# Two joints of a two-block transformer kernel, worked by halves of the tokens

## The chip, the cores and the metric

The kernel runs on one NeuronCore of a Trainium2 chip. The metric is the device time of one execution in microseconds (us); the time shown for a kernel is the median of its runs. The engines are called PE (TensorE), DVE (VectorE), ACT (ScalarE), POOL (GpSimd) and SP (SyncE, which here issues the loads).

## The reference

512 tokens of width 1024 go through two blocks, all in float32. The part that matters here begins inside the first block and ends inside the second:

```python
h2 = _modulate(_rmsnorm(x, norm2_g[l]), mod_l[3], mod_l[4])
x = x + mod_l[5] * _conv_ffn(h2, ...)          # its w_down: 2816 -> 1024
...
return _rmsnorm(x, final_norm_g)               # end of the first block
...
h = rms_norm(x, norm_mix_pre[l])               # second block
proj = h @ w_in[l]                             # begins with q and k, 1024 columns
...
x = x + rms_norm(merged @ w_out[l], norm_mix_post[l])
h = rms_norm(x, norm_ffn_pre[l])
u = causal_dwconv(h @ w_up[l], conv_ffn_w[l])  # 1024 -> 5632
a, g = jnp.split(u, 2, axis=-1)
f = (jax.nn.gelu(g, approximate=True) * a) @ w_down[l]
x = x + rms_norm(f, norm_ffn_post[l])
```

Between `w_down` of the first block and `w_in` of the second stand two norms in a row, and between `w_out` and `w_up` of the second stand two norms with a residual sum between them. At each of these joints every number of the next product depends on all 1024 features of its token.

## The kernel before, in words

Activations lie with the features on the 128 partitions, in KC = 8 chunks of 128, and the T = 512 tokens along the free side. A linear produces one block of 128 output features at a time in one PSUM bank of 512 columns. Each product in float32 precision is made of three matmuls (`product`, lines 551 to 554): both operands are split into a high part (float32r) and a low part (the rest), and high x low, low x high and high x high are added. So a block with 1024 inputs is 24 matmuls of 512 columns, and a block of the down projection with its 22 input chunks is 66.

**Weights.** `load_order` is one list of weight tiles of 128 x 1024 (or 896), in the order of use. SP loads each into one of RAW = 3 raw places (`load`, lines 2336 and before) as soon as the low part three tiles earlier is made (`s_lo`). ACT writes the high part (`prepare`, line 1202) and DVE the low part (`low`, line 1676), each into one of KEPT = 3 places; ACT waits for the tile three before to be used up by PE (`s_used`). The places in each engine's program where `prepare(n)` and `low(n)` stand are written by hand, so they are queued between that engine's other work, in order.

**Order.** Every engine runs one program written out in order (`tensor_program`, `scalar_program`, `vector_program`, `gpsimd_program`, `sync_program`), and they meet only through semaphores. Blocks of output rotate through banks 0 to 5 (`turn`), banks 6 and 7 (`NORM_BANKS`) hold norm sums and spread factors. A bank is taken again when what it held has been read (`freed`).

**A norm.** ACT squares the chunks, DVE adds the squares up (`add`, line 1693). PE sums over the partitions by matmuls against a column of ones (`sum_over_partitions`, line 628), which gives one number per token, the tokens on the partitions. ACT takes the root (`root`, line 1214), DVE the reciprocal (line 1697), and PE spreads the factors over a bank by a product with the identity (`spread`, line 642). DVE then multiplies each chunk (`plain`), ACT makes its high part (line 1217) and DVE its low part; PE starts with chunk k when its low part is there.

**Joint one** (before). After the eight down blocks PE forms the sums of the final norm (`n_final`) and of the squares times the final gain (`n_three`), whole. `n_three`'s factor is derived from both sums by DVE (lines 2098 to 2103), spread first, then `n_final`'s. DVE makes the eight chunks of h (lines 2115 and 2108), the first two of the eight q and k linears run side by side, chunk by chunk (`side_by_side`), and x times the final norm is written after that (line 2123).

**Joint two** (before). While the eight output blocks run, ACT squares each and copies it to `y_buf`, DVE adds. Then the sum and spread of `n_post`, `y_buf` times its factor (line 2209), the sum to x (line 2213, and for chunks 1 and 4 on POOL, line 2302), squares of the new x (ACT, line 1619), their addition in pairs on POOL (line 2306), `n_four`'s sum on PE over the pairs, its root and spread, the eight chunks (lines 2224 and 2218), and the first two of 44 up blocks side by side.

**The first block's own joint**, between its output and its up projection, is already by halves of 256 tokens: `half_steps` makes one half of a block with 24 matmuls of 256 columns, `side_by_side_halves` runs several blocks chunk by chunk on one half and calls sums and spreads of the other half between the chunks, and `piece` gives four half-wide places to the normed chunks. Its steps on DVE are lines 1923, 1989, 2001, 2009 and 2015, on ACT 1436, 1441 and 1446.

Of the kernel before, what the change touches and what calls it, by code (L numbers as in the profile page):

```python
# [13 lines left out]
P = 128  # L14
# [37 lines left out]
    ("conv_mix_w_2", AC * 3), ("conv_ffn_w_2", 2 * FC * 3), ("eps", 1), ("one", 1),  # L52
# [19 lines left out]
KEPT = 3  # L72
STICK = 5
# [190 lines left out]
def two_blocks(nc, io, out):  # L264
    with ExitStack() as whole:
# [19 lines left out]
        small = sb(whole, "small", [P, TT])  # L285
        std = sb(whole, "std", [P, 2 * TT])
# [44 lines left out]
        with ExitStack() as branch:  # L331
# [15 lines left out]
            with ExitStack() as merge:  # L347
                m_hi = sb(merge, "m_hi", [P, KC, T], F32R)
                m_lo = sb(merge, "m_lo", [P, KC, T], F32R)
                y_buf = sb(merge, "y_buf", [P, KC, T])  # L350
                pairs = sb(merge, "square_pairs", [P, 4, T])
# [45 lines left out]
        N_TILES = len(loads.tile_load)  # L397
        row_load = [i for i, entry in enumerate(loads.load) if entry[0] == "row"]
# [47 lines left out]
        n_final = NormSems(1)  # L446
        n_three, n_post, n_four = NormSems(0, factor=0), NormSems(1), NormSems(0)
        s_n3_both = semaphore("n3_both")
# [10 lines left out]
        h_one, h_two, h_three, h_four = (InputSems(*n) for n in ((0, 0, 0), (0, 1, 1), (2, 1, 3), (3, 1, 4)))  # L459
# [16 lines left out]
        s_x1f, s_x1n = semaphore("x1_ffn"), semaphore("x1_normed")  # L476
# [7 lines left out]
        s_y, s_yn, s_x2_v, s_x2_p, s_pair = (semaphore(n) for n in ("y", "y_normed", "x2_v", "x2_p", "pair"))  # L484
# [5 lines left out]
        s_y2, s_yn2, s_x3_v, s_x3_p = Count(s_y, KC), Count(s_yn, KC), Count(s_x2_v, KC - 2), Count(s_x2_p, 2)  # L490

        POOL_CHUNKS = (1, 4)

        def by_engine(k, vector, pool):

            if k in POOL_CHUNKS:
                return pool, POOL_CHUNKS.index(k) + 1
            return vector, k + 1 - sum(c < k for c in POOL_CHUNKS)

        def x2_by(k):  # L500
            return by_engine(k, s_x2_v, s_x2_p)
# [34 lines left out]

        def early_at(i):
# [5 lines left out]
        def tensor_program(e):  # L543
# [12 lines left out]
            def tile_of(t):  # L556
                e.wait_ge(s_lo, t + 1)
                return w_hi[:, t % KEPT, :], w_lo[:, t % KEPT, :]

# [416 lines left out]
            for o in range(KC):  # L976
# [3 lines left out]
            turn = (turn + KC) % 6  # L980
# [7 lines left out]
            freed[n_three.bank] = h_three.plain.at(KC)  # L988
            norm_spread(n_final, TT)
            freed[n_final.bank] = (s_x1n, KC)  # L990
# [3 lines left out]
            side_by_side(W["qk2"], (turn, (turn + 1) % 6), h_hi, h_lo, h_three.lo.sem, h_three.lo.chunk)  # L994
            for o in range(2 * AC):
                b = (turn + o) % 6
                if o >= 2:
                    linear(W["qk2"] + o, 1, b, h_hi, h_lo)
                freed[b] = (s_qk2, o + 1)
            turn = (turn + 2 * AC) % 6  # L1000
# [110 lines left out]
            for o in range(KC):  # L1111
# [3 lines left out]
                freed[b] = (s_y, o + 1)  # L1115
            turn = (turn + KC) % 6
            norm_sum(n_post, exact[:, 0, :], squares[:, 0, :], TT)
            norm_spread(n_post, TT)
            freed[n_post.bank] = (s_yn, KC)
            free(n_four.bank)  # L1120
            for k in range(KC):
                if k >= KC - 2:
                    e.wait_ge(*n_four.square.at(k + 1))
                    done = sum_over_partitions(n_four.bank, pairs[:, k % 4, :], TT, False, k == KC - 1)
                elif k % 2:
                    e.wait_ge(s_pair, k // 2 + 1)
# [1394 lines left out]
```

## Time and profile before

| | |
|---|---|
| median of 3 runs | 1445.42 us (1444.22 to 1450.18) |
| the profiled execution | 1444.88 us |
| its span in the profile | 1443.6 us |
| PE matmuls busy | 1384.5 us, 96% |
| DVE busy | 741.7 us, 51% |
| ACT busy | 598.8 us, 41% |
| POOL busy | 14.3 us, 1% |
| HBM traffic | 103 GB/s over the span |

Times in the rows are microseconds from the span's start, and a matmul's duration includes its way through the array: one starts every 0.23 us though each is shown with 0.39. In the profile's 40 slices of the span PE is at nine tenths or more in all but the first, the last and four others; two of these, the 29th and 30th at seven tenths, are joint two at 1032 to 1081. Joint one is at 665 to 678.

### The profile page before, as it was taken

What the parts mean: (1) busy time and instruction counts of PE and PEld (TensorE: products, weight loads), DVE (VectorE), ACT (ScalarE), POOL (GpSimd) and SP (SyncE); (2) the same over time, 40 slices, a digit from 0 to 9 for tenths busy, and PEclk for the clock granted to TensorE, in tenths of its full rate; (3) what the DMA queues carried; (4) which work ended last, traced back from release to release, by engine and by line L of the source; (5) the groups of instructions that cost most, each with busy time, mean ns of one, the idle gap of its engine ahead of it and who ended that gap; (6) DMA issues with size and microseconds to landing.
All of it is one profiled execution on the core that took longest, in us unless ns stands there. A gap on an engine that the chain in (4) does not pass through costs nothing.

```text
span 1443.6 us, 16617 instructions
## 1 busy us (share of the span) xinstructions
PE 1384.5 (96%) x6734; PEld 1123.9 (78%) x6734; DVE 741.7 (51%) x985; ACT 598.8 (41%) x835; POOL 14.3 (1%) x20
## 2 busy tenths in 40 slices
PE   6999988999999999999999999999779999999997
PEld 3777766888888888887887887888668888888886
DVE  5678855665554443334414444444466566654224
ACT  5646766353333333222344444334343344333221
POOL 0000000000000000000000000000100000000000
PEclk9999999999999999998999999999879999999998
DMA  9644322323432332331322221324103322333331
GB/s 382 260 142 139 108 70 84 106 80 131 140 138 92 98 97 81 99 103 45 106 85 73 74 73 37 95 88 125 65 26 110 99 88 88 102 99 94 94 94 59
DMA packets 43099, 150.41 MB, mean 104 GB/s; under 512 B 4752, under 2 KB 6928, under 8 KB 41872
## 3 DMA queue, kind: packets, MB, share of 16 engines
q1 hardware_dynamic: 42144, 144.76, 30.7%
q0 software_dynamic: 880, 4.59, 1.0%
q8 instruction: 54, 0.88, 0.3%
q14 instruction: 21, 0.17, 0.0%
HBM read 146.45 MB, written 2.10 MB: 103 GB/s over the span
## 4 chain that ended last, share of the span: by engine, by line
PE 90%; DVE 5%; ACT 2%; issue 1%; DMA 1%; POOL 0%; DVEq 0%; SPq 0%; ACTq 0%
PE banks L552 27%; PE banks L554 26%; PE banks L553 26%; PE banks L628 1%; PE banks L693 1%; PE banks L837 1%; PE banks L696 1%; PE banks L704 1%; PE banks L1054 1%; PE banks L1053 1%; PE banks L642 1%; PE banks L820 1%; PE banks L1045 1%; PE banks L1081 1%; PE banks L666 1%
## 5 line engine op out<-in xcount | busy, mean ns | idle before, releaser
L552 PE MATMUL banks<-h_lo,w_hi 128*128 128x512 f32 (+1 forms) x1224 | 480.0, 392 | 9.6 <-DVE h_lo L2015 3.1
L553 PE MATMUL banks<-h_hi,w_lo 128*128 128x512 f32 (+1 forms) x1224 | 475.0, 388 | 0.0
L554 PE MATMUL banks<-h_hi,w_hi 128*128 128x512 f32 (+1 forms) x1224 | 474.9, 388 | 0.0
L1676 DVE TENSOR_TENSOR w_lo<-raw_w,w_hi 128x1024 fp32r<-128x1024 f32 (+2 forms) x229 | 266.2, 1164 | 367.9 <-ACT w_hi L1202 367.4
L1202 ACT ACTIVATE w_hi<-raw_w 128x1024 fp32r<-128x1024 f32 (+2 forms) x229 | 230.1, 1006 | 240.3 <-PE banks L554 214.1
L552 PEld LDWEIGHTS banks<-h_lo,w_hi 128*128 128x128 f32 x1224 | 231.5, 189 | 66.2 <-issue 12.0
L554 PEld LDWEIGHTS banks<-h_hi,w_hi 128*128 128x128 f32 x1224 | 231.5, 189 | 50.5
L553 PEld LDWEIGHTS banks<-h_hi,w_lo 128*128 128x128 f32 x1224 | 231.8, 189 | 48.5
L552 PE MATMUL banks<-a_lo,w_hi 128*128 128x512 f32 (+1 forms) x374 | 142.7, 382 | 0.0
L554 PE MATMUL banks<-a_hi,w_hi 128*128 128x512 f32 (+1 forms) x374 | 142.2, 380 | 0.0
L553 PE MATMUL banks<-a_hi,w_lo 128*128 128x512 f32 (+1 forms) x374 | 141.6, 379 | 0.0
L554 PEld LDWEIGHTS banks<-a_hi,w_hi 128*128 128x128 f32 x374 | 70.2, 188 | 14.8
L553 PEld LDWEIGHTS banks<-a_hi,w_lo 128*128 128x128 f32 x374 | 70.3, 188 | 14.5
L552 PEld LDWEIGHTS banks<-a_lo,w_hi 128*128 128x128 f32 x374 | 70.3, 188 | 13.8
L1745 DVE SCALAR_TENSOR_TENSOR exact<-banks,cols_sb,exact 128x510 f32<-128x510 f32 (+1 forms) x44 | 33.0, 749 | 53.5 <-ACT exact L1635 52.7
L1745 DVE SCALAR_TENSOR_TENSOR normed<-banks,cols_sb,normed 128x510 f32<-128x510 f32 (+1 forms) x66 | 49.2, 746 | 3.2 <-ACT normed L1635 2.4
L1635 ACT ACTIVATE exact<-banks,cols_sb 128x512 f32<-128x512 f32 x22 | 15.2, 689 | 83.1 <-PE banks L554 83.1
L1217 ACT ACTIVATE a_hi<-normed 128x512 fp32r<-128x512 f32 x44 | 27.8, 633 | 47.2 <-DVE normed L2075 30.5
L1739 DVE SCALAR_TENSOR_TENSOR cv_acc<-cv_in,cols_sb,cv_acc 128x512 f32<-128x512 f32 x60 | 45.0, 749 | 1.2
L1923 DVE SCALAR_TENSOR_TENSOR x_res<-banks,mod,x_res 128x512 f32<-128x512 f32 (+1 forms) x23 | 16.1, 702 | 42.0 <-PE banks L554 42.0
L1483 ACT ACTIVATE normed<-normed 128x512 f32<-128x512 f32 x22 | 13.9, 632 | 54.8 <-DVE normed L2071 54.8
L2134 DVE SCALAR_TENSOR_TENSOR sp<-banks,sp 128x1024 f32<-128x1024 f32 (+1 forms) x8 | 11.9, 1492 | 41.9 <-ACT sp L1543 41.9
(284 smaller groups left out, 1411.0 us busy)
## 6 DMA issues: line engine op xcount, KB each, us to landing
raw_w<-in_w_ffn_up SPq DMA_DIRECT2D x44, 512.0 KB, 3.8
raw_w<-in_w_up SPq DMA_DIRECT2D x44, 512.0 KB, 3.8
raw_w<-in_ada_rows SPq DMA_DIRECT2D x24, 512.0 KB, 4.2
early<-in_ada_turned SPq DMA_DIRECT2D x8, 1024.0 KB, 16.3
raw_w<-in_w_gates SPq DMA_DIRECT2D x16, 512.0 KB, 3.6
raw_w<-in_w_ffn_down SPq DMA_DIRECT2D x16, 448.0 KB, 3.3
raw_w<-in_w_down SPq DMA_DIRECT2D x16, 448.0 KB, 3.3
raw_w<-in_w_conv SPq DMA_DIRECT2D x12, 512.0 KB, 3.6
```

The costliest lines, as they stand in the source:

```text
L552: e.matmul(dst, lhs_hi, rhs_lo, start=first, stop=False)
L553: e.matmul(dst, lhs_lo, rhs_hi, start=False, stop=False)
L554: return e.matmul(dst, lhs_hi, rhs_hi, start=False, stop=last)
L628: done = e.matmul(bank[b][:, t:t + 1], part[:, t * P:(t + 1) * P], ones[:, :], start=(first and t == 0), stop=(last and t == nt - 1), skip ...
L642: done = e.matmul(bank[b][:, t * P:(t + 1) * P], f[:, t:t + 1].to_broadcast([P, P]), identity, start=True, stop=True)
L1202: e.activation(w_hi[:, t % KEPT, 0:n], raw[:, i % RAW, 0:n], ACT.Copy).then_inc(s_hi, 1)
L1217: e.activation(dst, src, ACT.Copy).then_inc(done, 1)
L1635: e.activation(dst, bank[b[n]][:, :], ACT.Copy, scale=col("conv_ffn_w_2", w)).then_inc(s_up2_centre.sem, 1)
L1676: e.tensor_tensor(w_lo[:, s, 0:n], raw[:, i % RAW, 0:n], w_hi[:, s, 0:n].bitcast(F32), ALU.subtract).then_inc(s_lo, 1)
L1739: e.scalar_tensor_tensor(out=acc, in0=src, scalar=col("cv_w", i), in1=acc, op0=ALU.mult, op1=ALU.add).then_inc(s_tap_v, 1)
L1745: return e.scalar_tensor_tensor(out=y[:, shift:T], in0=src[:, 0:T - shift], scalar=w, in1=y[:, shift:T], op0=ALU.mult, op1=ALU.add)
L1923: e.scalar_tensor_tensor(out=x[:, o, tok], in0=bank[b][:, 0:tok.stop - tok.start], scalar=mod[:, gate + o:gate + o + 1], in1=x[:, o, tok], ...
```

## The change

At both joints the tokens are worked in two halves, and the sums of both norms of each joint are formed from what is known earlier.

- Joint one: the last down block is made for tokens 0 to 255, then for 256 to 511. The pre-norm's factor is taken from one sum, of squares with the gain sqrt(g^2 + eps), so that the final norm's sum is no longer needed for it. Its sum, root, reciprocal and spread are made per half, the first half's during the second half of the down block. Three linears are made by halves (the first two side by side). The final norm's own sum is moved behind linear three and its spread behind linear four, and x times the final norm after it; low parts of weight tiles stand between its chunks.
- Joint two: the last three output blocks are made first for one half of the tokens, then for the other. The sum of squares of the new x is no longer taken from it: with y the output times its gain and f the post norm's factor, it is the sum of x^2 (from joint one's factors, `x_total`), twice f times the sum of x y, and f^2 times the sum of y^2. So three sums run along with the output blocks: squares of the output, x times y (`cross`, DVE), squares of y. Per half PE sums them over the partitions, and both norms' factors are spread together. Five up blocks run side by side by halves.
- Weights: five more places (`late_hi`, `late_lo`) hold tiles of the output blocks 3 to 7 and of up blocks 3 to 5, in memory that the branches used, so `prepare` and `low` run up to six tiles ahead (`kept_at`).
- POOL no longer takes part in joint two.

The core of the diff (the same pattern for half 1 and plain renumbering of semaphores left out):

```diff
+        def kept_at(t):
+            n, ring = t - W["out2"], KC + 3
+            if n < 3:
+                return (w_hi[:, t % KEPT, :], w_lo[:, t % KEPT, :]), t - KEPT
+            if n < KC or ring <= n < ring + 3:
+                at = n - 3 if n < KC else n - ring
+                return (late_hi[:, at, :], late_lo[:, at, :]), W["out2"] - 1 if n < KC else t - KC
+            at = (W["out2"] + (n - KC if n < ring else n - ring - 3)) % KEPT
+            return (w_hi[:, at, :], w_lo[:, at, :]), t - KC if n < ring else t - 6 if n < ring + 6 else t - KEPT
...
 # PE, joint one
-            norm_sum(n_final, exact[:, 0, :], squares[:, 0, :], TT)
-            norm_sum(n_three, exact[:, 1, :], squares[:, 1, :], TT)
-            e.wait_ge(s_n3_both, 2)
-            spread(n_three.bank, small[:, 0:TT], TT).then_inc(n_three.spread.sem, 1)
-            norm_spread(n_final, TT)
-            side_by_side(W["qk2"], (turn, (turn + 1) % 6), h_hi, h_lo, h_three.lo.sem, h_three.lo.chunk)
+            for k in down_half(0):
+                pass
+            for k in down_half(1):
+                if k == 4:
+                    third_sum(0)
+                elif k == 6:
+                    third_spread(0)
+            tiles, places = [W["qk2"] + n for n in range(3)], [(turn + n) % 6 for n in range(3)]
+            side_by_side_halves(0, tiles[0:2], places, h_three.lo.sem, third_ready, None, {3: third_sum, 6: third_spread})
+            half_linear(tiles[2], places[2], 0, h_hi, h_lo)
+            for t, b in zip(tiles, places):
+                half_linear(t, b, 1, h_hi, h_lo, at=HALF, ready=h_three.lo.sem, need=third_ready, done=s_used)
...
+                if o == 3:
+                    sum_over_partitions(n_final.bank, exact[:, 0, :], TT, True, True).then_inc(n_final.sum.sem, 1)
+                elif o == 4:
+                    norm_spread(n_final, TT)
...
 # PE, joint two
+            for u in range(KC - 3, OUT_UNITS):
+                o, half = (u, 0) if u < KC else (u - 3, 1)
+                for j, _ in enumerate(half_steps(W["out2"] + o, b, half, m_hi, m_lo, done=s_used if half else s_late)):
+                    if (u, j) == (KC, 3):
+                        output_squares(0)
+                    elif (u, j) == (KC, 7):
+                        output_sums(0)
+                    elif (u, j) == (KC + 1, 7):
+                        output_spreads(0)
+            side_by_side_halves(0, tiles, places, h_four.lo.sem, fourth_ready, None, {1: output_squares, 2: output_sums, 6: output_spreads})
+            side_by_side_halves(1, tiles, places, h_four.lo.sem, fourth_ready, s_used, {})
...
 # ACT, per output block or half block
+                e.activation((parts_of if u else totals)[Y_SQUARES][:, tok], src, ACT.Square)
+                e.activation(y_buf[:, o, tok], src, ACT.Copy, scale=col("norm_mix_post_2", o))
+                e.activation((parts_of if u else totals)[SCALED_SQUARES][:, tok], src, ACT.Square, scale=col("norm_mix_post_2", o))
...
 # DVE, joint one
+            add_third(0)
+            add_third_squares(0)
+            third_factor(0)
+            third_plain(0, 0)
+            for k in range(1, KC):
+                third_plain(0, k)
+                third_lo(0, k - 1)
+                if k == 2:
+                    low(W["qk2"] + 1)
+                elif k == 3:
+                    low(W["qk2"] + 2)
+                elif k == 4:
+                    add_third(1)
+                elif k == 5:
+                    add_third_squares(1)
+                    low(W["qk2"] + 3)
...
 # DVE, joint two
+            for o in range(KC - 3):
+                low(W["out2"] + (7, 8, 10, 11, 12)[o])
+                output_unit(o)
+            low(W["up2"] + LATE_KEPT)
+            output_unit(KC - 3)
+            output_unit(KC - 2)
+            cross(KC - 1)
+            post_factor(0)
+            fourth_total(0)
+            fourth_factor(0)
+            output_unit(KC)
+            added_y(0, 0)
+            added_y(0, 1)
+            fourth_plain(0, 0)
+            low(W["up2"] + LATE_KEPT + 1)
+            for k in range(KC - 1):
+                if k + 2 < KC:
+                    added_y(0, k + 2)
+                fourth_plain(0, k + 1)
+                fourth_lo(0, k)
+                if k == 0:
+                    output_unit(KC + 1)
+                elif k == 2:
+                    cross(KC + 2)
+                elif k == 3:
+                    post_factor(1)
+                    fourth_total(1)
+                elif k == 5:
+                    fourth_factor(1)
+            added_y(1, 0)
+            added_y(1, 1)
+            fourth_lo(0, KC - 1)
...
 # POOL
-            add_chunk(1)
-            pair(1)
-            pair(3)
-            add_chunk(4)
-            pair(5)
```

`output_unit(u)` on DVE is one product (`cross`) and three additions into running sums; units 0 to 4 are whole output blocks, 5 to 7 the first halves of the last three and 8 to 10 their second halves. `added_y` multiplies a half chunk of y by the spread factor and then, after that has finished, adds it to x. `fourth_total` is five dependent operations on 128 x 2 elements.

## Rows read from the trace of the kernel before

**Rows 1.** The profile's chain of work that ended last, share of the span by engine.

```profile
PE 90%; DVE 5%; ACT 2%; issue 1%; DMA 1%; POOL 0%; DVEq 0%; SPq 0%; ACTq 0%
```

**Rows 2.** PE's timeline, joint one: start, duration, line, operation [idle before, releaser].

```profile
664.65 0.39 PE L554 MATMUL banks<-a_hi,w_hi 128*128 128x512 f32 x1
...
677.85 0.49 PE L552 MATMUL banks<-h_lo,w_hi 128*128 128x512 f32 x1 [0.68 <-DVE h_lo L2108]
```

**Rows 3.** PE's timeline, joint two.

```profile
1032.25 0.95 PE L628 MATMUL banks<-ones,exact 128*128 128x1 f32 x8
1033.10 1.05 PE L628 MATMUL banks<-ones,squares 128*128 128x1 f32 x8
...
1060.70 0.77 PE L552 MATMUL banks<-h_lo,w_hi 128*128 128x512 f32 x1 [2.32 <-DVE h_lo L2218]
...
1080.55 0.50 PE L552 MATMUL banks<-h_lo,w_hi 128*128 128x512 f32 x1 [1.49 <-DVE w_lo L1676]
```

**Rows 4.** Busy us by stretch: PE, PEld, DVE, ACT, POOL; then PEclk, DMA share, GB/s.

```profile
990.00:1033.00 43.00, 43.00 (x194) 35.40 (x192) 13.20 (x15) 15.64 (x24) 0.00 (x0) 1.00 0.28 94
1033.00:1060.00 27.00, 13.93 (x66) 13.03 (x65) 14.47 (x20) 7.41 (x15) 7.26 (x5) 0.56 0.07 20
1083.00:1200.00 117.00, 117.00 (x505) 94.87 (x504) 69.89 (x84) 46.10 (x61) 0.00 (x0) 1.00 0.32 100
```

**Rows 5.** PE's timeline, the first block's joint, already by halves.

```profile
275.15 0.28 PE L552 MATMUL banks<-h_lo,w_hi 128*128 128x256 f32 x1
...
282.85 0.28 PE L554 MATMUL banks<-h_hi,w_hi 128*128 128x256 f32 x1
284.36 0.58 PE L628 MATMUL banks<-ones,exact 128*128 128x1 f32 x4 [1.22 <-DVE exact L1989]
...
285.94 0.61 PE L642 MATMUL banks<-consts_sb,rstd 128*128 128x128 f32 x4
286.31 0.37 PE L552 MATMUL banks<-h_lo,w_hi 128*128 128x256 f32 x1
...
297.79 0.39 PE L552 MATMUL banks<-h_lo,w_hi 128*128 128x256 f32 x1 [2.11 <-DVE h_lo L2015]
...
300.13 0.41 PE L552 MATMUL banks<-h_lo,w_hi 128*128 128x256 f32 x1
...
302.05 0.41 PE L552 MATMUL banks<-h_lo,w_hi 128*128 128x256 f32 x1
```

**Rows 6.** Timelines of ACT and DVE: steps like the new ones, from four places.

```profile
284.97 0.26 ACT L1441 ACTIVATE std<-banks,cols_sb 128x2 f32<-128x2 f32 x1 [1.22 <-PE banks L628]
285.26 0.17 DVE L2001 RECIPROCAL rstd<-std 128x2 f32<-128x2 f32 x1 [1.05 <-ACT std L1441]
...
302.34 0.48 DVE L2009 SCALAR_TENSOR_TENSOR normed<-x_res,gain,banks 128x256 f32<-128x256 f32 x1
302.73 0.48 DVE L2015 SCALAR_TENSOR_TENSOR h_lo<-normed,mod,h_hi 128x256 fp32r<-128x256 f32 x1
...
650.41 1.28 DVE L1693 TENSOR_TENSOR exact<-exact,squares 128x512 f32<-128x512 f32 x2
...
998.80 0.60 ACT L1209 ACTIVATE exact<-banks 128x512 f32<-128x512 f32 x1 [5.38 <-PE banks L554]
999.30 0.59 ACT L1611 ACTIVATE y_buf<-banks 128x512 f32<-128x512 f32 x1
...
1434.75 0.48 DVE L2274 SCALAR_TENSOR_TENSOR y_buf<-y_buf,cols_sb,banks 128x256 f32<-128x256 f32 x1 [0.81 <-PE banks L642]
1435.26 0.42 DVE L2278 TENSOR_TENSOR x_res<-x_res,y_buf 128x256 f32<-128x256 f32 x1
1435.61 0.86 DVE L2274 SCALAR_TENSOR_TENSOR y_buf<-y_buf,cols_sb,banks 128x256 f32<-128x256 f32 x2
```

**Rows 7.** The profile's costliest groups: busy, mean ns of one | idle before, releaser.

```profile
L1676 DVE TENSOR_TENSOR w_lo<-raw_w,w_hi 128x1024 fp32r<-128x1024 f32 (+2 forms) x229 | 266.2, 1164 | 367.9 <-ACT w_hi L1202 367.4
L1202 ACT ACTIVATE w_hi<-raw_w 128x1024 fp32r<-128x1024 f32 (+2 forms) x229 | 230.1, 1006 | 240.3 <-PE banks L554 214.1
```

More of the change, by code:

```diff
@@ L72 @@
 KEPT = 3
+LATE_KEPT = 5
+OUT_UNITS = 11
 STICK = 5
@@ L975, in tensor_program @@
             turn = (turn + 2 * FC) % 6
-            for o in range(KC):
+            for o in range(KC - 1):
                 b = (turn + o) % 6
@@ L1114, in tensor_program @@
                     linear(W["out2"] + o, 1, b, m_hi, m_lo)
-                freed[b] = (s_y, o + 1)
-            turn = (turn + KC) % 6
[L1117 to L1126, printed above, removed]
-                    done = sum_over_partitions(n_four.bank, pairs[:, k % 4 - 1, :], TT, k == 1, False)
-                else:
-                    continue
-                done.then_inc(n_four.sum.sem, 1)
@@ L1131, in tensor_program, with output_sum @@
-            norm_spread(n_four, TT)
-            freed[n_four.bank] = h_four.plain.at(KC)
-            side_by_side(W["up2"], (turn, (turn + 1) % 6), h_hi, h_lo, h_four.lo.sem, h_four.lo.chunk)
+                freed[b] = n_four.square.at(o + 1)
+            SUMS_BANKS = (NORM_BANKS[1], (turn + KC - 1) % 6)
+            def output_sum(half, what):
+                for part in (totals[what], parts_of[what]):
+                    for n in range(NT):
+                        at = what * NT + n
+                        done = e.matmul(bank[SUMS_BANKS[half]][:, at:at + 1], part[:, (NT * half + n) * P:(NT * half + n + 1) * P], ones[:, :],
+                                        start=(at == 0 and part is totals[what]), stop=True, skip_group_check=True)
+                return done
@@ new lines, in output_spreads @@
+            def output_spreads(half):
+                free(NORM_BANKS[half])
+                e.wait_ge(*n_post.factor.at(half + 1))
+                e.wait_ge(*n_four.factor.at(half + 1))
+                for n, norm in enumerate((n_post, n_four)):
+                    for t in range(NT):
+                        i, columns = norm.at + NT * half + t, slice(HALF * n + t * P, HALF * n + (t + 1) * P)
+                        done = e.matmul(bank[NORM_BANKS[half]][:, columns], rstd[:, i:i + 1].to_broadcast([P, P]), identity, start=True, stop=True)
+                done.then_inc(n_post.spread.sem, 1)
@@ L1490, in scalar_program, with third_square @@
             e.preload_act_table(ACT.Sqrt)
-            for o in range(KC):
-                prepare(min(W["down"] + 3 * o + 5, W["qk2"] + 1))
+            def third_square(half):
+                tok = HALVES[half]
+                e.wait_ge(s_x1f, KC + half)
+                e.wait_ge(*n_three.add.at(KC - 2))
+                e.activation(squares[:, 1, tok], x[:, KC - 1, tok], ACT.Square, scale=both_gains[:, KC - 1:KC]).then_inc(n_three.square.sem, 1)
+                e.wait_ge(*n_final.add.at(KC - 2))
+                e.activation(squares[:, 0, tok], x[:, KC - 1, tok], ACT.Square).then_inc(n_final.square.sem, 1)
@@ L1506, in scalar_program @@
+            for k in range(KC):
+                third_hi(1, k)
             e.wait_ge(s_consts, 16)
```

431 lines of the change are left out of this document (313 added, 118 removed).

## The prediction

> **What bounds the kernel now.** I began with the chain of waits that ended last: TensorE (PE) carries 90% of it, so an edit pays only where PE stands still or does something other than products [rows 1]. Then PE's timeline at the two joints. At the first, the last 512-wide product of the down projection issues at 664.65 and the first of the next stage at 677.85; less the 0.23 that a product occupies, 12.97 us lie between them, filled with column sums, two spreads of factors and waits [rows 2]. At the second, sums begin at 1032.25, the first up product comes at 1060.70, and after 72 products there is one more wait for a low weight part, up to 1080.55 [rows 3]. In the later up blocks 505 products take 117.00 us [rows 4], 0.232 each; 72 are 16.7 us, so this joint costs 1080.55 - 1032.25 - 16.7 = 31.6 us. The stretches tell who could fill it: while the output blocks run, PE is full, but VectorE (DVE) is busy 13.2 of 43 us and ScalarE (ACT) 15.6 of 43 [rows 4]. That is the room into which the change moves norm work. In the second joint the granted clock falls to a mean of 0.56, that is to 1.2 GHz for most of it [rows 4].
>
> **The model for the new form** is already in this trace, at the first block's joint, which is written by halves. There 66 half-wide products issue from 275.15 to 282.85, 0.1185 us each [rows 5]. Two halves thus cost 0.237 against 0.232, 0.005 more; bounds are 0 and twice that, and I take 0.006, since the new halves pass more semaphore waits. A spread for a half takes 0.37 (285.94 to 286.31), and a pause of 2.11 us at 297.79 was followed by a stretch at 1.2 GHz in which half products issue every 0.213 us [rows 5]. For the issue gap, the Trainium skill ("TensorE: Matmul & The Clock Gate", Back-to-back issue gap) gives N/2.4 plus about 2.5 ns per matmul, so splitting would cost 0.0025 us a product, and the 330 split ones 0.8 us; the rows give more than twice that and the measurement is used.
>
> **Joint one, term by term.** Removed: the 12.97 us. Added on PE: (a) splitting the last down block (66 products) and three linears (72): 138 x 0.006 = 0.8. (b) The pre-norm's sums and spreads by halves: a sum for a full row of eight records takes 0.85 (1032.25 to 1033.10 [rows 3]), so a half 0.43, and a spread 0.37: 2 x 0.80 = 1.6. (c) The final norm's sum (0.85) and spread (0.75) now stand between linears three to five: 1.6. Its root, reciprocal and the eight writes of x follow beside whole 5.6 us linears, with DVE free. (d) Waits, from writing down the three engines' orders with row durations. Half 0 ends at 649.53 + 66 x 0.1185 = 657.4. add_gated half, square, add are three dependent half operations of 0.42 to 0.48 and end by 659.1, where PE's k = 4 is reached: no wait. The sum to the root takes 0.61 and to the reciprocal 0.9 (284.36 to 284.97 and 285.26) [rows 5, 6], so the factor is there at 660.4, at k = 6: 0.1. DVE has from 661.1 on for each chunk a plain (0.39 to the next start) and a low part (0.35) [rows 6], and among them three weight low parts of 1.16 and half 1's add. PE finishes the second half at 666.3 and finds four chunks ready. The add for the second sum is late by 0.6 (a square queued behind a hi part), chunk 5 by 1.0 (it stands behind the third weight low part), and the first linear's second half catches up with DVE at its end: 0.7. Sum 2.4. So 0.8 + 1.6 + 1.6 + 2.4 = 6.4, and the joint gives **6.5 us**.
>
> **Joint two.** Removed: the 31.6 us, with GpSimd's adds in it. Added on PE: (a) splitting three output blocks (72) and five up blocks (120): 192 x 0.006 = 1.2. (b) Per half: squares' sum (four matmuls, eight records) 0.85, cross and scaled squares 1.7, two norms' spreads 0.75; twice 3.3 = 6.6. This is more than the old sums' issue, since three sums are formed instead of two. (c) The hidden part: DVE now has for each whole block one product and three adds at a pitch of 0.6 (two adds in 1.28 [rows 6]), for each half unit the same at 0.35, and five more weight tiles of 1.16 (hi parts 1.0 on ACT) [rows 7]. With eight tiles from the first unit on this is 9.3 + 10.2 for the whole blocks + 4.6 for the halves = 24 us in the 33 from 1000 to 1033; ACT has three reads per unit at 0.5 to 0.6 [rows 6]. Both fit, but barely: a block has 5.5 us of PE, and 2.4 + 2 x 1.16 = 4.7 of DVE. Loads are issued three ahead, and the stage used 0.28 of the DMA engines for 8 tiles [rows 4]; 13 tiles make it 0.46: they fit. If this cover were gone, each late tile would show up as a wait of its own length, about 1.2. (d) The waits after the output. DVE needs per half and chunk a product and a dependent add to x (0.86 the pair [rows 6]), plain 0.39, low 0.35: 1.6 us, against PE's five blocks x 3 x 0.119 = 1.79. So DVE keeps pace except where something is queued in between. First chunk: the spread for half 0 comes after output block 6's second half, PE has 2.86 us more, DVE needs about 0.7 latency, two pairs 1.7, plain 0.4, one weight low part 1.1, another pair and plain 1.25: PE waits 2.3. Second chunk: unit 9's four half operations (1.4) are ahead of it: 1.1. Fifth chunk: DVE stands at the wait for half 1's sums, then five small dependent ones (1.0 at 0.2 each, bounds 0.17 to 0.3 [rows 6]): 1.1. Eighth: its low part is behind half 1's first two pairs, which wait for the spread that PE issues only one chunk before: 0.15 + 1.7 + 0.55: 2.4. Half 1 starts 0.2 late and then runs freely. Sum 7.1. (e) The clock. The pause of 2.11 us at 297.79 was followed by a fall; the one of 1.22 at 284.36 was not [rows 5]. Here two waits are of that size. A fall of that length slows about 15 half products by 0.213 - 0.119, 1.4 us. The first is partly absorbed in the wait after it, so I take 2.0 for both; bounds 0 and 2 x 1.4 per wait of over 1 us, 5.6. Together 1.2 + 6.6 + 7.1 + 2.0 = 16.9, and the joint gives **14.7 us**.
>
> After it the five blocks finished together have to be taken off their banks. There DVE is busy for 69.9 of PE's 117 us [rows 4], 6.7 per pair of blocks against 11.2 of PE, so it catches up and no bank is late: nothing.
>
> **Sum.** The profiled execution took 1444.88; 1444.88 - 6.5 - 14.7 = 1423.7. The median of the runs is 0.54 above it: **1424.2 us**. Bounds: without any wait and any fall of the clock 9.5 + 2.0 less, 1412.7; with all waits doubled and the clock's upper end 9.5 + 3.6 more, 1437.3.
>
> **Rivals.** *DVE order slips (1434).* For it: DVE runs at 85% of PE's time where three sums and weights come together, and a wait in one of its queues delays all behind it. Each wait twice as long is +9.5. Against: at the first block's joint the largest waits are 1.22 and 2.11 [rows 5]. *Waits vanish (1413).* My latencies may be too long; against it stand those same two waits. *The drained blocks hold PE (1430).* If the activation steps of blocks 0 to 4 fall behind, PE waits one block, +5.6, for a bank or a weight tile. *Slower: the clock stays at 1.2 GHz.* In the old second joint it stayed there for most of 27 us [rows 4]. If repeated short pauses kept it there through half 1 of the down block and three linears (210 half products) and through all five up blocks (240), it costs 450 x 0.094 = 42 us, and the time is about 1464. It decides from 225 half products at 1.2 GHz on, for 225 x 0.094 = 21.2. Against: one short episode only at the first block's joint. On this the Trainium skill (same page, A second HAM failure mode) speaks against the change: short idles between groups of matmuls can make the clock alternate between its levels. *The split does not start early:* if the second half's work is held by one semaphore of the first, joint two gives only half, 1431; nothing in the waits of the diff says so.
>
> **Numbers.** Forecast 0.70; slip 0.12; vanish 0.08; drained blocks 0.05; no early start 0.02; clock 0.03, of which 0.02 beyond 1452. A measurement here can tell 0.5%, 7.2 us, from no change: below 1438.2 is faster. All cases but the clock's, and 0.02 of the slip for one far longer than worked out, lie there: faster 0.95, same 0.03, slower 0.02. The range takes the forecast with a part of its neighbours: 1416 to 1433.
>
> **What would show it.** PE's timeline between the last down block and the next linears without a gap of over 1.2 us, 256-wide products at 0.119; the final norm's sum between linears; at joint two waits for h_lo of about 2.3 before the first chunk and before the eighth, and no w_lo wait in the output blocks or after the up blocks; no GpSimd work; granted clock at most one or two short falls. Wrong if PE waits for w_lo or for banks in the output stage, if a wait exceeds 4 us, or if 1.2 GHz lasts over 10 us.

## The result, and the profile of the changed kernel

The changed kernel takes **1413.64 us** (median of 4 runs, 1411.13 to 1416.29) against 1447.62 of the kernel before (4 runs, 1444.22 to 1450.18): ratio 0.9768, 95% interval 0.9749 to 0.9786. It is faster, as forecast, but the time lies below the range of 1416 to 1433: the gain is 34 us where 21.2 were forecast. The profiled execution took 1412.42.

First the joints, since the forecast was about them. The waits of TensorE (PE) in the changed kernel, from its timeline (start, duration, line, operation, idle before and releaser):

```profile
663.99 0.28 PE L582 MATMUL banks<-h_hi,w_hi 128*128 128x256 f32 x1
664.70 0.58 PE L656 MATMUL banks<-ones,exact 128*128 128x1 f32 x4 [0.43 <-DVE exact L2303]
...
666.75 0.38 PE L580 MATMUL banks<-h_lo,w_hi 128*128 128x256 f32 x1 [0.66 <-DVE h_lo L2322]
...
674.36 0.28 PE L582 MATMUL banks<-h_hi,w_hi 128*128 128x256 f32 x1
674.74 0.39 PE L580 MATMUL banks<-h_lo,w_hi 128*128 128x256 f32 x1
...
675.09 0.28 PE L582 MATMUL banks<-h_hi,w_hi 128*128 128x256 f32 x1
675.31 0.38 PE L580 MATMUL banks<-h_lo,w_hi 128*128 128x256 f32 x1
...
1001.38 0.28 PE L580 MATMUL banks<-m_lo,late_hi 128*128 128x256 f32 x1
...
1024.37 0.35 PE L580 MATMUL banks<-h_lo,w_hi 128*128 128x256 f32 x1 [2.03 <-DVE h_lo L2513]
...
1027.14 0.39 PE L580 MATMUL banks<-h_lo,w_hi 128*128 128x256 f32 x1 [0.76 <-DVE h_lo L2513]
...
1036.10 0.39 PE L580 MATMUL banks<-h_lo,w_hi 128*128 128x256 f32 x1 [0.67 <-DVE h_lo L2513]
...
1044.64 0.39 PE L580 MATMUL banks<-h_lo,w_hi 128*128 128x256 f32 x1 [2.10 <-DVE h_lo L2513]
...
1060.67 0.40 PE L580 MATMUL banks<-h_lo,late_hi 128*128 128x512 f32 x1
...
1083.01 0.50 PE L580 MATMUL banks<-h_lo,w_hi 128*128 128x512 f32 x1 [0.23 <-DVE w_lo L1871]
...
1090.16 0.50 PE L580 MATMUL banks<-h_lo,w_hi 128*128 128x512 f32 x1 [1.37 <-DVE w_lo L1871]
```

The long gaps of [rows 2, 3] are gone, and the forecast's waits are there, at their places: 0.43 for the second sum (0.6 forecast), then 2.03, 0.76, 0.67 and 2.10 for the first, second, fifth and eighth step of the second joint (2.3, 1.1, 1.1, 2.4). At the first joint the wait of 0.66 comes behind the third weight low part, as forecast with 1.0. The last two rows were not forecast. None of these is far enough off to make 13 us. The busy time by stretch, two stretches of the second joint and two outside it (columns as in [rows 4]), shows where to look:

```profile
350.00:500.00 150.00, 150.00 (x657) 123.09 (x656) 76.91 (x92) 55.26 (x70) 0.00 (x0) 1.00 0.35 122
990.00:1033.00 43.00, 40.21 (x293) 37.84 (x291) 31.82 (x69) 20.53 (x42) 0.00 (x0) 1.00 0.27 87
1033.00:1060.00 27.00, 24.23 (x203) 23.69 (x204) 16.95 (x49) 6.44 (x14) 0.00 (x0) 1.00 0.01 2
1083.00:1200.00 117.00, 115.62 (x504) 94.58 (x505) 75.18 (x90) 48.88 (x65) 0.00 (x0) 1.00 0.32 102
```

The joint is filled, at a granted clock of 1.00 where [rows 4] have 0.56. GpSimd has nothing to do there. DVE went from 13.20 to 31.82 us in the output stretch, the room that the forecast pointed at. But look at the last row: PE stood still for 1.4 us of it and still issued 504 products, against 505 with no idle time in [rows 4]. And the same look at a stretch that the change does not touch, the up projection of the first block, in the kernel before:

```profile
350.00:500.00 150.00, 150.00 (x647) 121.64 (x646) 77.26 (x95) 54.14 (x68) 0.00 (x0) 1.00 0.35 120
```

PE is full and at 2.4 GHz in both, and issued 647 products before, 657 after. One product costs 1.5% less, in stages whose code is the same. The pitch, the time from the issue of one 512-wide product to that of the next, is taken from successive issue times (a few records are missing, so this is better than the counts). It is 232.4 ns before and 228.9 ns after, in every stage that reads h. In the down stage it is 233.3 in both; in the stages that read a2, 228.9 in both. It goes by stage, and it is not the clock.

**A theory of places.** What differs in those stages is where tiles stand. The change puts `x_total` and `both_gains` ahead of `std`, and tiles are laid one after another in steps of 32 bytes, so the weight tiles move on by 64 bytes while h, which is allocated earlier, stays. The byte addresses in the two built programs:

```
            before   after
h_hi         32896   32896
h_lo         49280   49280
w_hi         94976   95040
w_lo        107264  107328
a_hi        123840  123904
a2_hi       119616  119680
```

Modulo 256, h stands 128 bytes on from w before and 64 after (pitch 232.4, 228.9); a 192 in both (233.3); a2 64 in both (228.9). The theory: the pitch of a 512-wide product depends on the distance of its moving operand from its weight tile, modulo 256 bytes. It is the distance and not the weights' place alone that these stages speak for: before, the weights stand at 0 modulo 256 for h, a and a2 alike, and the pitch is 232.4, 233.3 and 228.9. Rival: the pitch comes with the run or with the halves, and the change's own steps won all of it.

### The profile page after: what moved, and what is told of

It reads as the page before. It is cut to its first block, busy times and chain, and to the rows that moved or that the text cites. A ratio compares the mean times of both kernels' runs of the same rounds, so it can differ in the third digit from the quotient of the medians.

```text
span 1411.1 us, 17413 instructions
## 1 busy us (share of the span) xinstructions
PE 1362.0 (97%) x7040; PEld 1123.8 (80%) x7040; DVE 759.7 (54%) x1082; ACT 603.9 (43%) x866; POOL 7.0 (0%) x15
## 4 chain that ended last, share of the span: by engine, by line
PE 87%; DVE 8%; ACT 3%; issue 2%; DMA 1%; DVEq 0%; SPq 0%; ACTq 0%
PE banks L580 26%; PE banks L582 25%; PE banks L581 25%; ACT w_hi L1321 1%; DVE w_lo L1871 1%; PE banks L865 1%; PE banks L724 1%; PE banks L732 1%; PE banks L721 1%; PE banks L1127 1%; PE banks L1126 1%; PE banks L848 1%; PE banks L694 1%; PE banks L1118 1%; PE banks L1154 1%
## 5 line engine op out<-in xcount | busy, mean ns | idle before, releaser
L580 PE MATMUL banks<-h_lo,w_hi 128*128 128x512 f32 (+1 forms) x1248 | 473.6, 380 | 13.1 <-DVE h_lo L2513 5.6
L582 PE MATMUL banks<-h_hi,w_hi 128*128 128x512 f32 (+1 forms) x1248 | 470.0, 377 | 0.0
L581 PE MATMUL banks<-h_hi,w_lo 128*128 128x512 f32 (+1 forms) x1248 | 469.3, 376 | 0.0
L1871 DVE TENSOR_TENSOR w_lo<-raw_w,w_hi 128x1024 fp32r<-128x1024 f32 (+2 forms) x221 | 256.2, 1161 | 322.2 <-ACT w_hi L1321 319.9
L1321 ACT ACTIVATE w_hi<-raw_w 128x1024 fp32r<-128x1024 f32 (+2 forms) x221 | 221.4, 1004 | 235.1 <-PE banks L582 210.1
L580 PEld LDWEIGHTS banks<-h_lo,w_hi 128*128 128x128 f32 x1248 | 234.3, 188 | 65.8 <-issue 10.5
L582 PE MATMUL banks<-a_hi,w_hi 128*128 128x512 f32 (+1 forms) x396 | 146.2, 369 | 0.0
L581 PE MATMUL banks<-a_hi,w_lo 128*128 128x512 f32 (+1 forms) x396 | 145.8, 368 | 0.0
L581 PEld LDWEIGHTS banks<-a_hi,w_lo 128*128 128x128 f32 x396 | 74.5, 188 | 13.8
L580 PEld LDWEIGHTS banks<-a_lo,w_hi 128*128 128x128 f32 x396 | 74.4, 188 | 13.5
L582 PEld LDWEIGHTS banks<-a_hi,w_hi 128*128 128x128 f32 x396 | 74.4, 188 | 12.7
```

The lines of the kernel that those rows point to most:

```text
L580: e.matmul(dst, lhs_hi, rhs_lo, start=first, stop=False)
L581: e.matmul(dst, lhs_lo, rhs_hi, start=False, stop=False)
L582: return e.matmul(dst, lhs_hi, rhs_hi, start=False, stop=last)
L1321: e.activation(hi[:, 0:n], raw[:, i % RAW, 0:n], ACT.Copy).then_inc(s_hi, 1)
L1871: e.tensor_tensor(lo[:, 0:n], raw[:, i % RAW, 0:n], hi[:, 0:n].bitcast(F32), ALU.subtract).then_inc(s_lo, 1)
```

## The experiments

### The layout alone, with nothing of the change

One line in the kernel before; the second run has 32 in the place of 16.

```
+        sb(whole, "gap", [P, 16])
         std = sb(whole, "std", [P, 2 * TT])
```

> The kernel before with one unused tile of 64 bytes put ahead of std, so that the weight tiles raw, w_hi, w_lo and all tiles behind them lie 64 bytes further on, as the change lays them; h_hi and h_lo stay. Nothing else differs. Theory of the places: what one whole matmul of 512 columns costs depends on how far its moving operand lies from its weight tile, modulo 256 bytes. In the kernel before h stands 128 bytes on from w_hi and the whole products of the stages that read h came every 232.4 ns; in the changed kernel it stands 64 on and they came every 228.9 ns. So here 228.9 ns in the h stages, 233.3 instead of 232.2 in the second v projection, the other stages as before, and about 3,400 x 3.5 ns = 12 us less: 1436 us against 1447.6, both joints as long as before. Rival, the pitch is that of the run or comes with the halves, not with the places: 232.4 ns and no difference.

> The kernel before with an unused tile of 128 bytes ahead of std: the weight tiles move by 128 bytes and h then stands 0 bytes on from them modulo 256. Theory of the places: the few whole products of the changed kernel with this distance (blocks whose weights lie in the late tiles) came every 227.0 ns, so the h stages come every 227 ns, about 3,400 x 5.4 ns = 18 us less than before: 1429 us, 6 us below the kernel with 64 bytes. Rival one, any move off 128 does the same: 228.9 ns and 1436 us. Rival two, no effect of places: 1447 us.

Measured: 64 bytes **1435.35 us** (4 runs, 1434.08 to 1436.93), ratio 0.9914 [0.9899, 0.9928] to the kernel before at 1448.18 in the same series; 128 bytes **1428.71** (4 runs, 1427.60 to 1430.79), 0.9869 [0.9853, 0.9886]. The stretch of the up projection, 64 bytes and then 128 bytes:

```profile
350.00:500.00 150.00, 150.00 (x657) 123.09 (x656) 76.63 (x92) 55.20 (x70) 0.00 (x0) 1.00 0.36 122
```

```profile
350.00:500.00 150.00, 150.00 (x663) 124.26 (x662) 78.31 (x93) 55.73 (x70) 0.00 (x0) 1.00 0.36 122
```

657 products in 150 us is the changed kernel's count, without a line of the change. The pitch by issue times is 228.9 and 226.7 ns. An unused tile of 64 bytes is worth 12.8 us, one of 128 bytes 19.5. Both rivals fall: not every move does the same, and it is not the run.

### The change without the move

The changed kernel with `sb(whole, "gap", [P, 48])` ahead of `std`.

> The changed kernel with 192 unused bytes more ahead of std, so that h stands 128 bytes on from w_hi again, as in the kernel before; nothing else differs. Theory of the places: h stages at 232.4 ns again, about 12 us more than the changed kernel's 1413.6: 1425 us, which leaves some 22 us to the change as it is written. Rival, the change's own steps won all 34 us: 1414 us.

Measured: **1425.76 us** (4 runs, 1424.01 to 1427.29), ratio 0.9846 [0.9832, 0.9861], pitch 232.4 in the h stages. In the stretch of the up projection the count is again that of the kernel before:

```profile
350.00:500.00 150.00, 150.00 (x647) 121.63 (x646) 77.03 (x92) 54.24 (x68) 0.00 (x0) 1.00 0.35 120
```

So the change with the distances of before is worth 22.4 us, and the forecast of 1424.2 was in effect a forecast of this kernel.

This run also shows what the changed kernel's own profile does not, the fall of the clock. PE's timeline around the eighth step of the joint, then the two stretches behind the two long waits:

```profile
1051.83 0.38 PE L581 MATMUL banks<-h_lo,w_hi 128*128 128x256 f32 x1 [2.10 <-DVE h_lo L2514]
1052.05 0.27 PE L582 MATMUL banks<-h_hi,w_lo 128*128 128x256 f32 x1
1052.16 0.28 PE L583 MATMUL banks<-h_hi,w_hi 128*128 128x256 f32 x1
...
1053.21 0.41 PE L583 MATMUL banks<-h_hi,w_hi 128*128 128x256 f32 x1
1053.43 0.41 PE L581 MATMUL banks<-h_lo,late_hi 128*128 128x256 f32 x1
```

```profile
1031.00:1036.00 5.00, 4.73 (x29) 4.44 (x28) 4.90 (x15) 1.84 (x5) 0.00 (x0) 0.66 0.12 50
1051.00:1057.00 6.00, 5.17 (x31) 5.18 (x32) 5.89 (x16) 1.68 (x4) 0.00 (x0) 0.72 0.00 0
```

After a wait of 2.1 us the half products went from a pitch of 0.12 us (1052.05 to 1052.16) to 0.21 (1053.21 to 1053.43), for 16 of them. So it was after the other, where the next wait for h_lo shrank from 0.76 to 0.27, so that a part of the loss was absorbed, as forecast. That is the forecast's term (e), twice. In the changed kernel's profiled execution waits of 2.03 and 2.10 us were followed by none (1.00 in both stretches above).

The first block's joint, whose steps the edits leave alone, has a pause of 2.1 us of PE in all nine traces of the full kernels. In three of them (the kernel before, this one and the last of the study) the granted clock falls behind it, in six it does not. The stretch in the kernel before, then in the changed kernel:

```profile
296.00:303.00 7.00, 5.15 (x29) 4.91 (x30) 5.53 (x12) 3.69 (x8) 0.00 (x0) 0.76 0.22 76
296.00:303.00 7.00, 5.95 (x48) 5.76 (x49) 6.41 (x14) 3.48 (x8) 0.00 (x0) 1.00 0.22 76
```

The same pause is estimated to cost up to 1.4 us (15 half products by 0.094) in one execution and costs nothing in another; what decides it stays open. For the same reason the 12.1 us between this kernel and the changed one are not the pitch to the last digit; some 3,300 products by 3.5 ns are 11.5.

### The first joint alone

The hunks of the change that concern the down stage, the first-joint norms and the q and k linears, on the kernel before; the output stage, the second joint and the up blocks stay as they were, and the weight tiles stand as in the changed kernel.

```
-        n_three, n_post, n_four = NormSems(0, factor=0), NormSems(1), NormSems(0)
+        n_three = NormSems(0, square=KC + 1, add=KC, sum=2, root=2, factor=2, spread=2)
+        n_post, n_four = NormSems(1), NormSems(0)
...
+            for k in down_half(0):
+                pass
+            for k in down_half(1):
...
+            side_by_side_halves(0, tiles[0:2], places, h_three.lo.sem, third_ready, None, {3: third_sum, 6: third_spread})
```

> The change's first joint alone (last down block and three linears by halves, both totals of the norms as there), the second joint as before; the weight tiles stand where the changed kernel has them. Theory of the places with the first joint as forecast: 12 us from the places, 6.5 us from the joint: 1429 us; the first joint's granted clock stays at 2.4 GHz, where the kernel before fell at 667.8, so perhaps 1 to 2 us more. Rival, the first joint is worth the whole of what the forecast missed (19 us) and the places nothing: also 1428, told apart by the pitch (232.4 against 228.9 ns) and by the second joint's start: in the changed kernel up2+5 starts 350.4 us before the end, here block 5 as before.

Measured: **1426.86 us** (4 runs, 1425.76 to 1427.55), ratio 0.9854 [0.9839, 0.9868]. The pitch in the h stages is 228.9 ns, so the rival falls here too. That is 8.5 us below the kernel that has its layout alone, and 13.2 above the changed kernel. Medians of different executions differ in more than the joint, so the joints are better read inside one execution. Four steps stand at the borders: the last low part of a (ahead of the down stage), the last copy of k (behind the first joint), the last m_lo (ahead of the output stage) and the last copy of an up block (behind the second joint). The lines of these four steps, of which the last number before the semicolon is the start of the last one. Layout alone:

```profile
L2078 DVE TENSOR_TENSOR a_lo<-normed,a_hi x22: 691/693/694, 312.4 to 538.8; 128x512 fp32r<-128x512 f32 x22
...
L1520 ACT ACTIVATE k<-banks x4: 599/600/600, 700.3 to 716.8; 128x512 f32<-128x512 f32 x4
```

First joint alone:

```profile
L2160 DVE TENSOR_TENSOR a_lo<-normed,a_hi x22: 691/693/694, 310.5 to 536.9; 128x512 fp32r<-128x512 f32 x22
...
L1600 ACT ACTIVATE k<-banks x4: 598/600/600, 692.1 to 709.4; 128x512 f32<-128x512 f32 x4
...
L2326 DVE TENSOR_TENSOR m_lo<-gates,m_hi x8: 693/693/694, 898.9 to 976.4; 128x512 fp32r<-128x512 f32 x8
...
L1718 ACT ACTIVATE exact<-banks,cols_sb x22: 678/692/692, 1058.6 to 1290.3; 128x512 f32<-128x512 f32 x22
```

Both joints, the changed kernel:

```profile
L2438 DVE TENSOR_TENSOR m_lo<-gates,m_hi x8: 691/693/694, 900.4 to 977.9; 128x512 fp32r<-128x512 f32 x8
...
L1830 ACT ACTIVATE exact<-banks,cols_sb x22: 674/689/691, 1062.0 to 1277.2; 128x512 f32<-128x512 f32 x22
```

From a_lo to k the layout alone takes 716.8 - 538.8 = 178.0, with the first joint 172.5: it is worth 5.5 here, against 6.5 forecast and 8.5 between the medians. Of the rest 1.9 stand ahead of the down stage (538.8 against 536.9), where the edit does nothing; they are not the joint's, and where they come from stays open. From m_lo to the last up block it is 313.9 with the old second joint and 299.3 with the new: 14.6, against 14.7 forecast and 13.2 between the medians.

### The disputed cost by itself

A kernel that leaves the two blocks out and copies x to the output. PE multiplies one moving tile with 16 pairs of weight tiles, each 32 bytes nearer modulo 256; four blocks of 12 products per pair. A pass over the first four pairs comes ahead and is not counted.

```
        for d in PLACES:
            weights[d] = (sb(f"w_hi_d{d:03d}_", [P, CHUNKS * P], F32R), sb(f"w_lo_d{d:03d}_", [P, CHUNKS * P], F32R))
            sb(f"pad{d}", [P, 56])
...
                            e.matmul(dst, w_hi[:, w], m_lo[:, j, 0:n], start=j == 0, stop=False)
                            e.matmul(dst, w_lo[:, w], m_hi[:, j, 0:n], start=False, stop=False)
```

> The disputed cost by itself; the two blocks are left out, the output is the input x. One moving tile of four chunks, high and low part, and 16 pairs of weight tiles that each stand 32 bytes (modulo 256) nearer, so that the moving operand stands 0, 32, ... 224 bytes on from the weights and the eight distances come twice, in other places. With each pair four blocks of 12 products of 512 columns, in the order (hi, lo), (lo, hi), (hi, hi) of the kernel; then all again with 256 columns, then again with 512 in falling order. Theory of the places: at 512 columns 227 ns at a distance of 0, 229 at 64, 232.4 at 128, 233.3 at 192, the same in both places and in either order of time; what 32, 96, 160 and 224 give is not known, in between if the cost grows evenly. At 256 columns 117.8 at 64 and about 120 at 0 and 128, by the halves of the first stages. Rival, what counts is not the distance but where the weights stand, or something that the stages have besides: one pitch for all 16, since only the weights' place changes here and nothing else does, or one that does not repeat from the first eight to the second.

It took 530.9 us in all, one execution. The first product with each of the first five pairs, in PE's timeline; from one row to the next it is 48 products:

```profile
76.19 0.40 PE L298 MATMUL banks<-m_lo,w_hi_d_ 128*128 128x512 f32 x1
...
87.11 0.39 PE L298 MATMUL banks<-m_lo,w_hi_d_ 128*128 128x512 f32 x1
...
98.31 0.39 PE L298 MATMUL banks<-m_lo,w_hi_d_ 128*128 128x512 f32 x1
...
109.30 0.39 PE L298 MATMUL banks<-m_lo,w_hi_d_ 128*128 128x512 f32 x1
...
120.51 0.39 PE L298 MATMUL banks<-m_lo,w_hi_d_ 128*128 128x512 f32 x1
```

At 0 the 48 take 10.92 us, at 32 they take 11.20, at 64 10.99, at 96 11.21. From the issue times inside each group, rising, in the second eight places, and falling again:

```
distance, bytes mod 256      0      32     64     96     128    160    192    224
512 columns, ns, rising     226.9  233.3  229.0  233.4  233.2  234.3  233.3  233.4
  second eight places       226.7  233.3  229.0  233.4  233.2  234.3  233.3  233.4
  falling (first eight)     226.7  233.3  228.8  233.4  232.4  234.3  233.4  233.3
256 columns, ns             119.9  116.6  117.8  120.0  118.7  117.3  113.3  118.5
  second eight places       120.0  116.6  117.8  120.0  118.7  117.3  113.3  118.5
```

At 512 columns the theory holds: the pitch follows the weights' place modulo 256 and repeats after 256 bytes (128 alone differs with the order, 233.2 and 232.4). This kernel never moves the moving operand, so it can't tell the distance from the weights' own place; the stages of the full kernels do, where weights at 0 go with three pitches and distance 64 gives 228.9 with weights at 0 (a2 before) and at 64 (h after). The pitch does not grow evenly: two distances are cheap, 0 and 64, and the other six cost 2.5 to 3.4% more than 0.

At 256 columns the order is another, and in the full kernels the distance alone does not settle it. The halves of the down stage stand at 192 both in the changed kernel and in the one at the old distance; by issue times they come every 117.8 ns in the first and every 113.6 in the second. What decides between the two was not found.

### Two steps of the second joint moved

```
-            ... {1: output_squares, 2: output_sums, 6: output_spreads})
+            ... {1: output_squares, 2: output_sums, 4: output_spreads})
...
             fourth_plain(0, 0)
-            low(W["up2"] + LATE_KEPT + 1)
...
                     post_factor(1)
+                    low(W["up2"] + LATE_KEPT + 1)
                     fourth_total(1)
```

> The changed kernel with two steps of the second joint moved. TensorE spreads the second half's factors after chunk 4 of the five up blocks' first half instead of after chunk 6, and VectorE splits the seventh up weight tile after the second half's post factor instead of ahead of the first chunk of h_lo. In the changed kernel TensorE waited 2.03 us for the first h_lo chunk, behind that split (1.14 us on VectorE), and 2.10 us for the first chunk of the second half, which is worked out only after the spread. Theory, the chain of VectorE sets both waits: 1.1 us less of the first and the 2.1 us wait gone, with half a us of it back as a wait elsewhere: 2.6 to 3.7 us less than the changed kernel, 1410.5 us. Rival, the waits only move (VectorE is busy throughout, and the weight split then comes late for the block that needs it): 1413 to 1414 us.

Measured: **1408.68 us** (5 runs, 1408.02 to 1410.24), ratio 0.9733 [0.9716, 0.9750]; 5.0 below the changed kernel's median, 4.4 between the profiled executions (1412.42 and 1408.02). What PE waited for in it (us in total, times, longest):

```profile
PE banks L580 <- DVE h_lo L2513: 2.3, 3, 0.9
PE banks L580 <- DVE w_lo L1871: 1.6, 2, 1.4
```

In the changed kernel the first row reads 5.6, 4, 2.1. The waits went, 3.3 us, and did not come back elsewhere; the second row is as it was. So both were set by the order of DVE's and PE's queues, as the forecast's steps said, and could be had by reordering. (The expectation calls the chunk behind the 2.10 us the first of the second half; in the order of PE's program it is the eighth of the first half, whose low part DVE makes after two pairs of the second.) The 1.1 to 1.7 us beyond 3.3 were not traced.

### Every distance made 0, and one step further

On the kernel with the moved steps: `gap` [P, 16] ahead of `std`, [P, 48] behind `silu_c`, [P, 32] ahead of `a_hi`; then h, a, a2, att, cnv and m all stand 0 from the weights.

> The kernel with the two moved steps (e_tuned), and unused tiles that put h, a, a2, att, cnv and m all 0 bytes on from w_hi and w_lo, modulo 256: 64 bytes ahead of std, 192 behind silu_c, 128 ahead of a_hi. Theory of the places, with the table measured by itself (226.8 ns at 0, 228.9 at 64, 233.3 at 192): some 4,200 whole products lie at 64 now and gain 2.1 ns each, 8.9 us; the 462 whole products of the down stage, at 192 now, gain 6.5 each, 3.0 us; some 700 halves of 256 columns go from 117.8 to 119.9 ns and give back 1.5: 1408.7 - 10.4 = 1398 us. Rival, TensorE's quicker products only meet the other engines' work and weights sooner, and wait: 1403 to 1408 us.

Measured: **1397.89 us** (5 runs, 1397.44 to 1400.66), ratio 0.9669 [0.9654, 0.9684]; the best of the study. The stretch of the up projection, and one of the down projection:

```profile
350.00:500.00 150.00, 150.00 (x664) 124.20 (x663) 78.16 (x93) 55.20 (x69) 0.00 (x0) 1.00 0.34 120
550.00:640.00 90.00, 90.00 (x408) 74.92 (x408) 31.04 (x35) 24.33 (x31) 0.00 (x0) 1.00 0.33 97
```

664 against 657 (the second stretch has some halves in it and can't be compared by its count); the pitch by issue times is 226.7 in both, where the changed kernel has 228.9 and 233.3. The sum of the expectation, worked out from the table, was 1398.

The last kernel added [P, 16] ahead of `late_hi` and [P, 24] ahead of `hc_hi`.

> e_zero with two more places: the late weight tiles 64 bytes further on, so that m and h stand 192 bytes on from them, where 256 columns cost 113.3 ns (119.9 at 0), and the context's hc_hi and hc_lo 96 bytes further on, 192 from w_hi and 64 as the weight of the context's v. Theory of the places: 240 halves of the second joint gain 6.6 ns each, 1.6 us, the 72 whole products with late weights lose 6.5 each, 0.5 us, the context's halves gain 4 ns each, 0.4 us: 1.5 us below e_zero, 1396.5 us. In the second joint the half products may only run into the waits for h_lo, which VectorE sets: then no more than 0.5 us below e_zero.

Measured: **1399.09 us** (4 runs, 1398.38 to 1400.08), ratio 0.9669 [0.9656, 0.9683]: not below e_zero. PE's groups over the output stage and the second joint, shapes apart, products of m_lo with late weights; first e_zero, then the last kernel (count, busy us and mean ns of one):

```profile
L583 PE MATMUL banks<-m_lo,late_hi 128*128 128x512 f32 x16 | 6.2, 389 | 0.0
```

```profile
L585 PE MATMUL banks<-m_lo,late_hi 128*128 128x512 f32 x16 | 6.3, 396 | 0.0
```

With late weights at 192 a 512-wide product lasts 396 ns against 389, as expected. One step failed: by issue times most halves came every 117.8 ns (of 137 gaps with m_lo and m_hi only 27 were 113 or 114) and not every 113.3, so 240 x 2.1 ns won back only what the whole products lost. Here too the small kernel's 113.3 for distance 192 does not carry over; at 0 both agree on 119.9.

## Why the prediction was right on the change and wrong on the time

**The step that failed is the sum**: "1444.88 - 6.5 - 14.7". It took all products outside the joints to cost what they cost before. The diff shows two new tiles, `x_total` and `both_gains`, ahead of `raw`, `w_hi` and `w_lo`; the sum did not read them as a move of all weights by 64 bytes. That is worth 12.8 us by the layout alone and 12.1 by the change with and without it, and it is the whole difference: 21.2 and 12.8 make the measured 34.0. The hint was in the trace of before: its stages did not have one pitch. The stretch 1083 to 1200 [rows 4] gave 0.232 a product, while stages that read a2 had 0.229, and the forecast used one number without asking for the difference. The rule of the Trainium skill that it did weigh ("TensorE: Matmul & The Clock Gate", Back-to-back issue gap, N/2.4 plus about 2.5 ns, which the section gives for isolated matmuls) makes an estimate of 215.8 ns for 512 columns; the runs show 226.7 to 234.3, and the measurement decides.

**Joint one**: 6.5 forecast, 5.5 inside one execution. Its waits came about as written down: 0.43 for 0.6 at the second sum, 0.66 for 1.0 behind chunk 5, and the catching up with DVE at the end as pauses too short to be listed as waits. From 674.02 to 675.77 nine half products take 1.75 us where 9 x 0.118 are 1.06, so 0.7 for 0.7. Together 1.8, against 2.4. The term that was off is the time removed: 12.97 us in the trace of before, but only 11.7 in the kernel with the layout alone (last down product at 660.15, first of h at 672.08, less 0.23), where the clock fell later in the old sums.

**Joint two**: 14.7 forecast, 14.6 inside one execution, 13.2 between medians. The number is right by luck, since four errors cancel. The four waits were each mis-sized by 0.3 to 0.4, 7.1 forecast and 5.6 measured. The clock's 2.0 did not occur in the changed kernel's profile and did, twice, in the kernel at the old distance. The term was read from one execution, and the other traces show that it is no rule. Its upper bound of 5.6 counts two waits, though the forecast itself lists four over 1 us. Against these stands a term set at nothing, "DVE ... catches up and no bank is late: nothing": no bank was late, but two weight tiles were, 0.23 and 1.37 us, in the blocks after the joint, where DVE's low parts come late for PE. And splitting cost more than its 1.2. From the first half product to the next whole one (1001.38 to 1060.67) it is 59.3 us; less 192 products of 0.229, the waits of 5.6 and the sums and spreads of 6.7 (6.6 forecast), some 3 remain. So 16.9 was forecast as added, and 15.3 + 1.6 = 16.9 came, made up otherwise.

**The rivals.** 1413.64 is the number of the rival "waits vanish (1413)", and it would be wrong to book it there: the waits are in the trace, 5.6 us at the second joint. A time that agrees with a rival does not show its mechanism. The slip (waits shorter than forecast, not twice as long), the clock at 1.2 GHz throughout (1.00 in both stretches of the joint) and the split that does not start early are refuted by the rows above. The drained blocks came in part: no wait for a bank, but 1.6 us for weight tiles where the rival had 5.6, and a w_lo wait after the up blocks is what the forecast said would not be seen.

## What to carry to other kernels

A change that adds a tile moves every tile allocated after it. Before forecasting such a change, or judging one measured, compare the product pitch of a stage that it does not touch; if that has moved, subtract the layout first by running the kernel before with an unused tile of the same size. And choose the places: with moving operand and weights at equal addresses modulo 256 bytes, good for 512-wide products and not for 256-wide ones, three unused tiles gave 10.8 us here (1408.68 to 1397.89), half of what the whole rewrite of two joints gave.

## What the hardware showed that I had not expected

- The pitch of a 512-wide fp32r product at 2.4 GHz is 226.7 to 234.3 ns, by the distance of moving operand and weight tile modulo 256 bytes: 226.8 at 0, 228.9 at 64, 232.4 to 234.3 at the other multiples of 32. At 256 columns it is 113.3 to 120.0, with another order, and 0 is among the worst; there one distance (192) gave 117.8 in one full kernel and 113.6 in another.
- A pause of PE of 2.1 us at one and the same place was followed by some 15 half products at 1.2 GHz in three of nine traces and by none in six.
- What causes the dependence on the distance was not tried. Weights are loaded while PE is busy (123.09 us of loads in 150.00 us of full PE), so a collision of the two reads would fit; no run here tells it from another cause.
